# A two-layer, twice-over transformer stack on one core: the recurrence's eight two-column sums of squares dealt out over three chunks, in unused columns of a score bank

## The reference, cut to what matters

```python
kk = (k * k_k).reshape(B, S, H, N).astype(jnp.float32)
kk = kk / jnp.maximum(jnp.linalg.norm(kk, axis=-1, keepdims=True), 1e-12)
...
def step(state, inp):
    r_t, w_t, k_t, v_t, kk_t, a_t = inp
    sk = jnp.einsum('bhvk,bhk->bhv', state, kk_t)
    state = state * w_t[:, :, None, :] - sk[..., None] * (kk_t * a_t)[:, :, None, :] + v_t[..., None] * k_t[:, :, None, :]
    return state, jnp.einsum('bhvk,bhk->bhv', state, r_t)
```

## Time and profile before

| | us |
|---|---|
| median of 3 runs | 4260.09 (4253.25 to 4288.84) |
| the profiled execution | 4255.36 |
| its span, first to last instruction | 4253.6 |
| stretch of the recurrence, first step's r to the last's, in the span | 1399 to 2037 |
| mean granted TensorE clock over the span | 0.91 |

### The profile page before, as it was taken

How to read it: one execution, slowest core, us unless ns; L and a number is a source line. 1 busy time by engine, 2 the same in 40 slices (tenths; PEclk the granted TensorE clock), 3 DMA queues, 4 the chain that set the end, 5 groups by cost and what they waited for, 6 DMA issues and landing times. The chain is left out here.

```text
span 4253.6 us, 48223 instructions
## 1 busy us (share of the span) xinstructions
PE 3758.1 (88%) x18866; PEld 3044.6 (72%) x18866; DVE 2016.2 (47%) x3934; ACT 1703.1 (40%) x3132; POOL 107.6 (3%) x120
## 2 busy tenths in 40 slices
PE   6999679889995999999788999999788999998789
PEld 5888337668883777777666777777676688877666
DVE  3143323354335667775334455555544355565441
ACT  3222461344332333342234444444433465655420
POOL 0011120000000000000000000000000000000000
PEclk9999799989995777788899999999898999999789
DMA  3333302212222121121321111010122111110310
GB/s 125 114 127 114 111 0 80 85 45 94 103 76 74 40 63 40 40 50 40 124 79 41 33 31 31 26 36 21 45 90 80 63 32 40 35 35 11 134 50 40
DMA packets 219642, 265.62 MB, mean 62 GB/s; under 512 B 62620, under 2 KB 142612, under 8 KB 218392
## 3 DMA queue, kind: packets, MB, share of 16 engines
q1 hardware_dynamic: 219416, 262.53, 18.9%
HBM read 191.95 MB, written 70.52 MB: 62 GB/s over the span
## 5 line engine op out<-in xcount | busy, mean ns | idle before, releaser
L320 PE MATMUL bank<-wh,XH 128*128 128x512 f32 x1344 | 556.1, 414 | 55.9 <-DVE wl L304 38.2
L320 PE MATMUL bank<-wh,XL 128*128 128x512 f32 x1344 | 530.3, 395 | 0.0
L320 PE MATMUL bank<-wl,XH 128*128 128x512 f32 x1344 | 530.0, 394 | 0.0
L2325 PE MATMUL bank<-XH,wh 128*128 128x512 f32 x1040 | 427.2, 411 | 32.1 <-DVE wl L2314 19.8
L2325 PE MATMUL bank<-XH,wl 128*128 128x512 f32 x1040 | 411.5, 396 | 0.0
L2325 PE MATMUL bank<-XL,wh 128*128 128x512 f32 x1040 | 410.7, 395 | 0.0
L320 PEld LDWEIGHTS bank<-wh,XH 128*128 128x128 f32 x1344 | 257.0, 191 | 126.0 <-issue 50.7
L304 DVE TENSOR_TENSOR wl<-raw,wh 128x1024 fp32r<-128x1024 f32 x128 | 155.6, 1235 | 312.8 <-ACT wh L295 311.6
L320 PEld LDWEIGHTS bank<-wh,XL 128*128 128x128 f32 x1344 | 257.4, 192 | 60.4 <-issue 10.0
L320 PEld LDWEIGHTS bank<-wl,XH 128*128 128x128 f32 x1344 | 256.5, 191 | 56.1
L320 PE MATMUL bank<-XH,wh 128*128 128x512 f32 x704 | 278.7, 396 | 5.9 <-DVE XL L1435 5.9
(11 more groups left out here) (401 smaller groups left out, 7367.2 us busy)
## 6 DMA issues: line engine op xcount, KB each, us to landing
sc_zt<-stage SPq DMA_DIRECT2D x88, 256.0 KB, 2.0
raw<-in_att_w_in SPq DMA_DIRECT2D x33, 512.0 KB, 4.2
raw<-in_even_w_in SPq DMA_DIRECT2D x32, 512.0 KB, 5.1
raw<-in_odd_w_in SPq DMA_DIRECT2D x32, 512.0 KB, 4.7
raw<-in_rec_w_in SPq DMA_DIRECT2D x32, 512.0 KB, 4.0
sc_h<-H SPq DMA_DIRECT2D x24, 512.0 KB, 2.6
H<-sc_h SPq DMA_DIRECT2D x24, 512.0 KB, 7.8
sc_z<-stage SPq DMA_DIRECT2D x40, 256.0 KB, 2.0
```

The lines of the kernel that those rows point to most:

```text
L320: done = e.matmul(out, lhsT, rhs, start=k == 0 and j == 0, stop=k == NK - 1 and j == 2)
L2325: done = e.matmul(bank[:, :], x[:, k, :], y[:, k, ts], start=k == 0 and j == 0, stop=k == NK - 1 and j == 2)
```

## The change

1. ScalarE's kk and squares leave "scan" and become an entry "squares" of their own, right after lora 0, at the end of n = 2, one step earlier than before. "scan" stays where it is and is VectorE's alone.
2. The sixteen matmul instructions of "norm" become entries "norms" of chunks 0 to 2, 3 to 5 and 6 to 7 of pair p + 2, in n = 3, 4 and 5, each right after u and ahead of the next chunk's scores.
3. They write into columns 384 to 399 of bank 4, the scores' bank of the first head, which the scores leave free, instead of a bank of 0 and 1. For that, the norms wait until the mask of the step's scores has been read, ScalarE's square root waits until the mask of chunk 6 has been read, and the scores of chunk 7 (in step 6) wait for the square root.
4. The entry "norm" (ScalarE's square root, VectorE's floor and reciprocal) moves from the end of n = 4 to n = 5, behind tail 3 and ahead of the last solve.
5. Ahead of the steps, pair 0's squares come between lora 0 and lora 1; pair 1's order stays.

```diff
-    some(0, "load", "values", "gates", ("lora", 0), ("lora", 1), "scan", "norm", "spread", "centre", "unit", "key", "exps", "be", "al")
+    some(0, "load", "values", "gates", ("lora", 0), "squares", ("lora", 1), "scan", ("norms", 0, 8), "norm", "spread", "centre", "unit", "key", "exps", "be", "al")
...
-    ahead = {0: ["scan"], 8: ["norm"], 11: ["spread", "centre"], 16: ["unit"], 21: ["key", "exps"], 27: ["be", "ka"]}
+    ahead = {0: ["squares", "scan"], 8: [("norms", 0, 8), "norm"], 11: ["spread", "centre"], 16: ["unit"], 21: ["key", "exps"], 27: ["be", "ka"]}
...
         order.append(("chain", p, n, "u"))
+        if 3 <= n <= 5:
+            some(p + 2, ("norms", 3 * n - 9, min(3 * n - 6, 8)))
         if after:
             order.append(("scores", *after))
...
         elif n == 5:
             order.append(("tail", p, 0, 3))
+            some(p + 2, "norm")
...
         elif n == 2:
-            some(p + 2, ("lora", 0))
+            some(p + 2, ("lora", 0), "squares")
...
         elif n == 4:
-            some(p + 2, "norm")
             order.append(("tail", p, 0, 2))
...
-        if what in ("norm", "tokens"):
+        if what == "tokens":
             return [(what, p, *rest)]
...
-        elif what == "norm":
-            key = (what, p)
+        elif what == "norms":
+            first, end = rest
             e.wait_ge(*self.scaled.at("squares", p))
             if p == 0:
                 e.wait_ge(*self.tables.at("heads2"))
-            wait_all(e, self.bank_free(key))
-            for n in range(NS):
-                done = e.matmul(self.bank(*key)[:, 2 * n:2 * n + 2], self.t[:, self.chunk(n)], self.cols2[:, :], start=True, stop=True)
-            done.then_inc(*self.side.up(what, p))
+            if p >= 2:
+                e.wait_ge(*self.masked.at(p - 2, 3 + first // 3, 0))
+            elif p == 1:
+                e.wait_ge(*self.root.at(0))
+            for n in range(first, end):
+                done = e.matmul(self.c.banks[4][:, 3 * P + 2 * n:3 * P + 2 * n + 2], self.t[:, self.chunk(n)], self.cols2[:, :],
+                                start=True, stop=True)
+            done.then_inc(*self.side.up("norm", p, end))
...
         if n == 0:
             e.wait_ge(*self.fact.at("rh", p))
+            if p == 0:
+                e.wait_ge(*self.root.at(1))
+        if n == NS - 1 and p + 2 < 8:
+            e.wait_ge(*self.root.at(p + 2))
...
-        elif what == "scan":
+        elif what == "squares":
             e.wait_ge(*self.rk.at(p))
...
         elif what == "norm":
-            e.wait_ge(*self.side.at(what, p))
-            e.activation(self.nr[:, :], self.bank(what, p)[:, 0:2 * NS], ACT.Sqrt).then_inc(*self.root.up(p))
+            e.wait_ge(*self.side.at(what, p, NS))
+            if p >= 2:
+                e.wait_ge(*self.masked.at(p - 2, 6, 0))
+            e.activation(self.nr[:, :], self.c.banks[4][:, 3 * P:3 * P + 2 * NS], ACT.Sqrt).then_inc(*self.root.up(p))
```

More of the change, by code:

```diff
@@ L1697, in bank_free @@
             return []
-        flag = {"lora": self.sig, "norm": self.root, "unit": self.prep, "bonus": self.bonused, "alike": self.alone,
+        flag = {"lora": self.sig, "unit": self.prep, "bonus": self.bonused, "alike": self.alone,
                 "tokens": self.tokens, "tail": self.out}[former[0]]
```

## The result

The changed kernel takes 4303.58 us (median of 8 runs, 4298.23 to 4322.67), the one before 4262.98 in the same job (8 runs, 4247.24 to 4288.84): a ratio of 1.0090 with a 95% interval of 1.0067 to 1.0113, so 29 to 48 us more, inside the 1% that the prediction set as its bound for no change. Of the 18.6 us above the forecast, 7.6 are the base: the sum was made on one profile of before (4255.4), and the median of this job is 4262.98. The profiled execution took 4307.13 (span 4305.3), 51.8 above the profiled one of before.

What follows compares the result with a forecast made beforehand. PE was taken to bound steps 3, 5 and 6, VectorE step 4. On the profiled 4255.4 us, -2.0 + 5.4 + 3.9 + 17.0 + 6 = +30.3 gave 4285; range for eight in ten 4255 to 4304.

Steps and rivals of the forecast that it cites:

- The sign: Whole kernel: the change makes it slower, by +30.3 us in sum.
- the chain behind the root: Step 5: table load and root delay the last solve, `pt`'s store and T's loads by about 3.6 us.
- Step 4: Losing the norms' lump and the wait for R gains 0, far end -0.5, since VectorE's 12.71 us cover it.
- Norms in step 3: Six norm instructions ahead of the scores cost 1.34 us in each of pairs 1 to 4: 5.4 us.
- Squares in pairs 0 and 5: Step 3: early squares delay R, with norms 2.3 us in pair 0 and 1.6 in pair 5: 3.9 us.
- The root in step 5: Exposed table load and late solve delay T and X by 2.8 us a pair, norms included: 17.0 us.
- Clock in steps 5 and 6: New idle moments of PE make its clock rise later: +1 us a pair, 6 in all.
- Ahead of the steps: Pair 0's squares before lora 1 let its norms begin earlier: -2.0 us, between -2.5 and 0.
- the lost-clock case: Rival: clock stays half through step 6, +3 us a pair, +3 in pair 0's step 3; +46 us, 4301; chance 0.17.
- absorbed: Rival: X and the exps behind step 5 have room for the delay; +11 us, 4266; chance 0.18.
- The rival by which the kernel becomes faster: Clock stays high from step 5's start, shortening steps 5 and 6; -8 us, 4247; chance 0.10.

Runs made afterwards that it cites:

- e5: Kernel before, with only the squares of pair p + 2 moved to step 2's end, norms untouched: 1.0048, 4285.36 us.
- e4: Changed kernel with all sixteen norm instructions in step 4, behind u, the root still in step 5: 1.0043, 4285.21 us.
- r1: The kernel before, run once more unchanged for a second profile: 4267.64 us.
- e6: Kernel before, with only pair 0's squares moved ahead of lora 1, before the steps begin: 0.9984, 4265.52 us.
- e9: Changed kernel with squares in their old place, all norms behind u in step 4, table preloaded there, root at step 5's end: 1.0009, 4270.9 us.
- e10: Kernel before, with only the sixteen norm instructions moved within step 4 from its end to behind u: 1.0061, 4289.02 us.
- e1: Changed kernel with the norm entry (root, floor, reciprocal) moved to step 5's end, behind the last solve and S: 1.0072, 4301.21 us.
- e11: Changed kernel with the last solve put with the three before it, ahead of u in step 5: 1.0046, 4289.49 us.
- e3: Changed kernel with root's table loaded at step 4's end by an extra root, and norm moved behind S in step 5: 1.0046, 4283.33 us.
- e2: Changed kernel with an extra ScalarE root at step 4's end, so that the table is loaded there: 1.0050, 4291.31 us.

## Why the prediction was right, and where it was short

The sign and the chain behind the root hold: +30 was forecast, +38 (interval 29 to 48) measured. That 4303.58 still lies in the range, 0.4 us below its top, is luck: base and sum were both low. Term by term, with the ledger's means in place of single profiles (5 for the norms, 8 for pairs 0 and 5, 24 for steps 5 to 7, less 4 ahead of the steps: 33):

- **Step 4, 0:** right. 84.2 and 85.2 before, 85.1 and 85.2 after, VectorE's 12.71 unchanged; R's wait and the lump went into the wait for S.
- **Norms in step 3, 4 x 1.34 = 5.4:** right. Pairs 1 to 4 sum to 60.6 and 60.9 with them, to 55.0 and 56.1 without (e5, e4).
- **Squares in pairs 0 and 5, with their norms 3.9:** the term that failed. Those two steps sum to 30.3 in after, to 21.9 on the mean of before, r1, e6, e9 and e10 (17.8 to 25.6): +8. The wait for R was forecast at 1.6 in pair 0 and is 1.24; in pair 5, forecast at 1.2, it isn't there in after's first profile and is 0.37 in the second. What was under-sized is the clock, which the prediction put aside as a far end of +3 in pair 0 alone. Against the one profile that the prediction read it is +12, but some 4 of these are that profile's luck: 9.16 us and a clock of 1.00 in pair 5 came once in six profiles. The step that failed is thus the reading of one execution's clock as a property of the step. By the medians, squares alone (e5) cost 20 us, with an interval of 8 to 33; its ledger has 12 more than the old place's means (6.5 in step 3, 5.2 in steps 5 to 7), inside that interval. Its profile has 8 to 12 more in pairs 6 and 7, too, which the edit doesn't touch.
- **The root in step 5, with the norms 17.0:** right in its steps, too large as waiting. From F's copy to the last solve's end 2.7 were forecast (3.6 less 0.89) and 2.34 measured, since the root starts before `vars` has ended; S ends 1.4 later; X starts on average 2.1 us later behind F's copy than before (7.70 to 9.82, six pairs; forecast 2.8 less 0.89). One statement was incomplete: T's loads don't hang on the last solve alone. Behind it, 1.1 us apart, comes `ptt`'s store in the same queue, which e1 and e11 brought to light.
- **Clock in steps 5 and 6, 6:** under-sized. Root, load and clock together are right: 17.7 forecast (17.0 less 5.3 for the norms, plus 6), 20.4 measured by e3. Their split is not. Over steps 5 to 7 PE's idle time grew only from 5.8 to 11.9 us (means of before, r1 and e6, and of after's two), 6 where the forecast had 11.7; its busy time grew by 18, of which the norms are 5.3 by the prediction's own estimate. So some 13 us are the same matmuls at a lower clock, twice the 6 of the forecast: the mean clock of step 6 is 0.79 to 0.85 in the three and 0.71 and 0.75 in the two. That the two errors cancel is luck.
- **Ahead of the steps, -2.0:** short; about -3.8 is measured, beyond the far end of -2.5. From the first lora product to the first r it is 97.3 and 96.9 us in two profiles of before, 93.4 and 93.2 of after. PE's norms start 2.9 us earlier there. Pair 0's squares alone (e6) give 95.6, so 1.5 us; where the rest comes from isn't shown.

Two sums in the prediction are rounded up (6 x 2.8 is 16.8, not 17.0; the lost-clock case adds up to 45.3, not 46), and PE's idle time in step 7 stands in the trace (1.0 us a pair), but not in the earlier trace rows. None of this moves the forecast.

Of the rivals, "absorbed" fell with X's waits, and "the clock is lost" came true in part: pair 2's step 6 took 15.12 us at 0.50 in the first profile of after and 11.48 in the second. The rival by which the kernel becomes faster exists as a mechanism: e9 runs step 5 at full clock in all pairs, e10 at 0.90 or more, e4 in three of six. In them all sixteen norm instructions stand behind u in step 4, where PE is then busy for 13.4 to 13.6 us in pair 3 instead of 12.2; the change leaves six there. Even so it brings nothing (e9, e10), since T's round trip or VectorE's queue is late next.

The Trainium skill (ScalarE: Activation LUTs, "What ACT_TABLE_LOAD costs") would have had 1.4 us of drain besides the load. The load here starts 0.02 us behind F's copy, and `vars` 0.01 behind the load: 1.28 and no more. The trace doesn't agree with the drain, and the sum was right to leave it out.

What stays open: what decides, in pair 0's step 3, whether the clock falls when order and idle time are as before (8.61 in four, 13.20 and 13.49 in two), and with it how much of the 0 in eight with the early squares is due to them; and the exact shares of e1, e2 and e11, whose ratios differ from after's by 8, 17 and 19 us, each plus or minus some 14. The score bank was never tried alone; e9, which has it, can't be told from before. No version here beats the kernel before by more than its interval.

## What to carry to other kernels

Taking work out of a stretch helps only if its engine bounds the stretch; otherwise look at what the work covered, and at the bound of where it goes. The lump of norms lay in PE's wait for S and covered a table load; its parts now stand in steps that PE bounds. When a wait is moved off one queue, read the next: T's loads stood behind two stores with different producers, and only both repairs together (e3) freed them. And before a step's length in one profile enters a sum, see whether a second execution repeats its clock.

## What the runs showed that had not been expected

TensorE can stay at 1.2 GHz while its records leave no gap: pair 2's step 3 of after has 15.93 us busy of 15.93 at a mean granted clock of 0.50. Most of these matmuls have few columns (2, 64 or 128). And in pair 0's step 3 the same 56 instructions, after steps with the same order, took 8.61 us at 1.00 in some kernels and 13.2 to 13.5 at 0.61 to 0.62 in others. The Trainium skill (TensorE: Matmul & The Clock Gate, "What's actually happening") says that the clock's bookkeeping runs freely and doesn't start with the kernel, so that one kernel measures differently by where its start falls; the scatter here would fit that, with pair 5's step 3 of the same kernel at 9.16 and 12.86 us, but no run here varies the start by itself, so it isn't shown. The same section's sentence that activity releases the throttle doesn't suffice to tell these rows: the records are full, and the clock is halved.

Second, the place of sixteen two-column matmuls within a step that VectorE bounds can change the clock of the next one: with them at step 4's end step 5 ran at 0.50 to 0.66 in all pairs of before, r1 and e6, with the same sixteen behind u at 1.00 (e9) and 0.90 to 1.00 (e10). With the squares early too (e4) it did so in three pairs of six.
